# Third block's dense products in a long f32 kernel: seven half-width products for a pair of feature tiles where there were eight

## The reference

```python
def even_layer(h, w_in, conv_w, sgu_ln_g, sgu_ln_b, sgu_w, sgu_b, w_out):
    p = jnp.einsum('bsd,de->bse', h, w_in)
    xa, ba, ca, za, ub, vb, zb = jnp.split(p, EVEN_SPLITS, axis=-1)   # seven parts of 1024
    ya = short_conv_branch(xa, ba, ca, conv_w) * jax.nn.silu(za)      # ba * conv3(ca * xa)
    yb = chunked_sgu_branch(ub, vb, ...) * jax.nn.silu(zb)            # ub * (w_s @ layer_norm(vb) + b_s)
    return jnp.einsum('bse,ed->bsd', jnp.concatenate([ya, yb], axis=-1), w_out)

def odd_layer(h, w_in, ...):
    p = jnp.einsum('bsd,de->bse', h, w_in)
    pc, zc, fd, zd = jnp.split(p, ODD_SPLITS, axis=-1)    # pc: 3200 wide, for a head scan
    ...

def third_block(x, ...):
    h = x
    h = h + even_layer(rms_norm_3(h, e_norm_g), ...)
    h = h + odd_layer(rms_norm_3(h, o_norm_g), ...)
    return rms_norm_3(h, final_norm_g)
```

## Time and profile before

| | us |
|---|---|
| median of 3 runs (lowest to highest) | 5252.62 (5249.73 to 5260.67) |
| the profiled execution's own time | 5247.91 |
| its span, first to last instruction | 5246.1 |
| of it TensorE busy | 4898.0 |
| VectorE busy | 2250.8 |
| ScalarE busy | 886.0 |

### The profile page before, as it was taken

How to read it: one execution, slowest core, us unless ns; L and a number is a source line. 1 busy time by engine, 2 the same in 40 slices (tenths; PEclk the granted TensorE clock), 3 DMA queues, 4 the chain that set the end, 5 groups by cost and what they waited for, 6 DMA issues and landing times.

```text
span 5246.1 us, 54331 instructions
## 1 busy us (share of the span) xinstructions
PE 4898.0 (93%) x23372; PEld 3331.0 (63%) x23372; DVE 2250.8 (43%) x3820; ACT 886.0 (17%) x1530; POOL 146.6 (3%) x228
## 2 busy tenths in 40 slices
PE   8999999889999998999999999899998888888988
PEld 7885445774556885565564788444444777777743
DVE  5674874431214465553441655311011555555402
ACT  0001113120111002212221100100001333333211
POOL 0000000000000000000000000000000111111100
PEclk9998999989999998999999999999999999999999
DMA  6523340013222221112111221222221000000021
GB/s 233 174 88 51 66 71 31 1 33 72 96 73 74 87 91 46 49 41 65 41 33 64 81 89 65 80 74 71 72 72 36 1 1 1 1 1 1 17 91 40
DMA packets 284911, 311.51 MB, mean 59 GB/s; under 512 B 7168, under 2 KB 277632, under 8 KB 281472
## 3 DMA queue, kind: packets, MB, share of 16 engines
q1 hardware_dynamic: 284672, 308.04, 19.9%
HBM read 305.92 MB, written 2.10 MB: 59 GB/s over the span
## 4 chain that ended last, share of the span: by engine, by line
PE 52%; DVE 4%; ACT 3%; issue 0%; DMA 0%; SPq 0%; DVEq 0%; ACTq 0%
PE ps L262 24%; PE ps L338 7%; PE ps L748 4%; PE ps L761 2%; PE ps L735 1%; PE ps L1931 1%; PE ps L2621 1%; PE ps L307 1%; PE ps L456 1%; PE ps L2639 1%; PE ps L768 1%; PE ps L1650 1%; PE ps L2382 1%; PE ps L1639 1%; PE ps L2860 1%; PE ps L2552 1%
## 5 line engine op out<-in xcount | busy, mean ns | idle before, releaser
L262 PE MATMUL ps<-main,w 128*128 128x512 f32 (+1 forms) x4976 | 2161.3, 594 | 71.5 <-DMA w<-in_ffn_wg 19.1
L262 PEld LDWEIGHTS ps<-main,w 128*128 128x128 f32 x4976 | 949.1, 193 | 1206.8 <-issue 1177.2
L338 PE MATMUL ps<-main 128*128 128x256 f32 x2992 | 665.6, 380 | 0.0
L338 PEld LDWEIGHTS ps<-main 128*128 128x128 f32 x2992 | 569.7, 190 | 76.1
L338 PE MATMUL ps<-main,w 128*128 128x256 f32 x2264 | 504.5, 380 | 0.0
L338 PEld LDWEIGHTS ps<-main,w 128*128 128x128 f32 x2264 | 431.1, 190 | 58.8 <-issue 1.4
L748 PE MATMUL ps<-main,w 128*128 128x128 f32 x1536 | 226.5, 297 | 4.0 <-DVE main L2725 2.2
L748 PEld LDWEIGHTS ps<-main,w 128*128 128x128 f32 x1536 | 204.5, 208 | 16.4 <-issue 5.7
L602 DVE SCALAR_TENSOR_TENSOR main<-main,params_sb 128x512 f32<-128x512 f32 x256 | 192.5, 752 | 9.1
L781 ACT COPY main<-ps 128x512 f32<-128x512 f32 x180 | 105.5, 586 | 509.8 <-PE ps L735 509.8
L761 PE MATMUL ps<-main 128*128 128x128 f32 x1440 | 181.9, 280 | 2.4 <-DVE main L807 2.4
(11 more groups left out here) (446 smaller groups left out, 4762.7 us busy)
## 6 DMA issues: line engine op xcount, KB each, us to landing
w<-in_w_in SPq DMA_DIRECT2D x58, 1024.0 KB, 6.2
w<-in_e_w_in SPq DMA_DIRECT2D x28, 1024.0 KB, 5.1
main<-in_ada_w SPq DMA_DIRECT2D x24, 1024.0 KB, 4.9
w<-in_ffn_wg SPq DMA_DIRECT2D x22, 1024.0 KB, 6.3
w<-in_ffn_wu SPq DMA_DIRECT2D x22, 1024.0 KB, 6.4
w<-in_o_w_in SPq DMA_DIRECT2D x20, 1024.0 KB, 5.3
w<-in_ffn_wd SPq DMA_DIRECT2D x16, 1024.0 KB, 5.1
w<-in_w_up SPq DMA_DIRECT2D x16, 1024.0 KB, 5.4
```

Source lines behind the costliest of these rows:

```text
L262: i = pe.mm(PS[b][:, 0:n], wv[:, k, f * 128:(f + 1) * 128], g.X(kg + k), start=kg + k == 0, stop=kg + k == g.nk - 1)
L338: t = pe.mm(PS[b][:, 256 * half:256 * half + 256], weight[:, m, :], x(m), start=m == 0, stop=m == n - 1)
```

## The change

All products of the even layer and p are made by the seven-product step, but for the first pair of v, of x and of p, and p's last single tile, which stay plain. Even input: 26 steps. Even output: the 16 input tiles are taken as two groups of 8 (kg 0 and 8), each a step of its own whose result is added to `X`: 8 steps. p: 11 steps. The order of the input products stays; in the output product groups of 0 and 8 interleave. ScalarE's copies of tiles go, and `act_seven`'s copies come; Silu works on two tiles at once, in place, behind the results. VectorE gets the halves, the weights' differences (made two steps ahead) and the results, which `dve_seven_out` can now write to tiles 514 apart (`stride`).

```diff
-    def dve_seven_out(v, g, j, kg, out):
+    def dve_seven_out(v, g, j, kg, out, stride=TOK):
...
-    G_even = {n: Gemm("even " + n, e_in, k * D, 8, 8, H3, ("rms", "even"))
+    G_even = {n: Gemm("even " + n, e_in, k * D, 8, 8, H3, ("rms", "even"), seven=(*ES, EX, ("even x",)))
...
+    def even_steps():
+
+        e = [(G_even["v"], j, 0) for j in (2, 4, 6)]
+        e += [(G_even[n], j, 0) for j in range(0, 8, 2) for n in "xcbz"][1:]
+        e += [(G_even[n], j, 0) for n in "us" for j in range(0, 8, 2)]
+        return e + [(G_eout, j, kg) for j, kg in ((0, 0), (2, 0), (0, 8), (2, 8), (4, 0), (4, 8), (6, 0), (6, 8))]
...
-        run(pe_gemm(pe, G_even["v"]))
+        steps = even_steps()
+        run(pe_pair(pe, G_even["v"], 0))
+        for step in steps[0:3]:
+            run(pe_seven(pe, *step))
         pe_ln(pe, "sgu", between=lambda pe: run(pe_pair(pe, G_even["x"], 0)))
-        for j in range(0, 8, 2):
-            for n in "xcbz" if j else "cbz":
-                run(pe_pair(pe, G_even[n], j))
+        for step in steps[3:18]:
+            run(pe_seven(pe, *step))
...
+        def silu(g, j):
+            a.wait_ge(*at("out", "seven", 3, g.name, j, 0))
+            a.act(U3.ap, U3.ap, ACT.Silu).then_inc(a.inc(s, "out", g.name, j), 1)
+        for g, j, kg in steps[3:18]:
+            act_seven(a, g, j)
+            if g is G_even["z"]:
+                silu(g, j)
...
+            if g is G_even["c"]:
+                if used:
+                    v.wait_ge(*at(*used))
+                dve_seven_out(v, g, j, 0, 33800)
+                for f in (j, j + 1):
+                    v.wait_ge(*at("out", "even x", f))
+                v.wait_ge(*at("out", "seven", 3, g.name, j, 0))
+                v.tt(src.ap[:, :, 1:513], src.ap[:, :, 1:513], EO, MUL).then_inc(v.inc(s, "even xc", j), 1)
+                v.wait_ge(*at("even xc", j))
+                for f in (j, j + 1):
+                    dve_conv(v, s, ("conv3", f), Y3(f), src(f % 2), 3, lambda i: par("e_conv_w_3", 8 * i + f))
...
+            weights_of(n + 2)
...
+        dve_out = {4: (0, 1), 5: (2, 3), 7: (4, 5)}
+        for n, (g, j, kg) in enumerate(steps[26:], 26):
+            v.wait_ge(*at(*used))
+            dve_seven_out(v, g, j, kg, 33800)
...
+            v.tt(X.ap[:, j:j + 2, :], X.ap[:, j:j + 2, :], EO, ADD).then_inc(v.inc(s, *done, j), 1)
+            v.also(*done, j + 1)
+            used = (*done, j)
+            for f in dve_out.get(n - 26, ()):
+                dve_total_squares(v, "odd", f)
+            weights_of(n + 2)
+        for f in (6, 7):
+            dve_total_squares(v, "odd", f)
...
-        run(pe_gemm(pe, G_p))
+        run(pe_pair(pe, G_p, 0))
+        for j in range(2, 24, 2):
+            run(pe_seven(pe, G_p, j))
+        run(pe_pair(pe, G_p, 24))
```

More of the change, by code:

```diff
@@ L2263, in pe_even @@
             t.then_inc(pe.inc(s, "mm", "sgu", f), 1)
-        run(pe_gemm(pe, G_even["u"]))
-        run(pe_gemm(pe, G_even["s"]))
-        run(pe_gemm(pe, G_eout))
+        for step in steps[18:]:
+            run(pe_seven(pe, *step))
     def act_even(a):
@@ L2270, in act_even @@
         act_rms(a, "even", X, x3)
-        for f in range(8):
+        for f in range(2):
             a.wait_ge(*at("mm", "even v", f))
             a.copy(V3(f), bank("even v", f)).then_inc(a.inc(s, "out", "even v", f), 1)
+        steps = even_steps()
+        for step in steps[0:3]:
+            act_seven(a, *step)
         act_ln(a, "sgu", V3, "e_sgu_ln_g_3", "e_sgu_ln_b_3")
[L2275 to L2287, removed]
+        a.wait_ge(*at("pad3", 0))
+        for f in range(2):
+            a.wait_ge(*at("mm", "even x", f))
+            a.copy(pad3[0].ap[:, f, 1:513], bank("even x", f)).then_inc(a.inc(s, "out", "even x", f), 1)
+        def silu(g, j):
[5 more added lines that the diff above has]
+                silu(g, j)
         for f in range(8):
@@ L2290, in act_even @@
             a.copy(t512[f], bank("sgu tp", f)).then_inc(a.inc(s, "out", "sgu tp", f), 1)
[L2291 to L2294, removed]
+        for g, j, kg in steps[18:26]:
+            act_seven(a, g, j)
+            if g is G_even["s"]:
+                silu(g, j)
+        act_out = {3: (0, 1), 4: (2, 3), 6: (4, 5)}
+        for n, step in enumerate(steps[26:]):
+            act_seven(a, *step)
+            for f in act_out.get(n, ()):
+                act_square(a, "odd", X, x4, f, True)
+        for f in (6, 7):
+            act_square(a, "odd", X, x4, f, True)
     def dve_even(v):
@@ L2350, in assemble @@
     DD, DS, FW = mem(26162, 1, 256), mem(26418, 8), mem(30514, 4, 128)
-    G_p = Gemm("p", o_in, 0, 25, 8, H3, ("rms", "odd"))
+    G_p = Gemm("p", o_in, 0, 25, 8, H3, ("rms", "odd"),
+               seven=([mem(25138 + 2048 * i, 4) for i in range(2)], [mem(29234 + 256 * i, 1, 256)(0) for i in range(2)],
+                      pairs_at(*range(21042, 25138, 1024)), ("odd x",)))
     G_f = Gemm("f", o_in, 4224, 4, 8, H3b, ("rms", "odd 2"))
@@ L2473, in dve_odd @@
         v.fill(PP.ap[:, :, 513:514], 0.0).then_inc(v.inc(s, "pp pad"), 1)
+        for m in range(4):
+            dve_halves(v, ("odd x",), H3, G_p.seven[2], m, ("rms", "odd"))
+        for j in (2, 4):
+            dve_seven_weights(v, G_p, j)
+        for j in range(2, 24, 2):
+            dve_seven_out(v, G_p, j, 0, 8193 + 514 * j, 514)
+            for f in (j, j + 1):
+                v.also("out", "p", f)
+            if j < 20:
+                dve_seven_weights(v, G_p, j + 4)
         v.fence("p")
```

139 lines of the change are left out of this document (95 added, 44 removed).

## The result

The changed kernel takes 5203.52 us (median; 5193.92 to 5205.35), the kernel before, run beside it, 5251.17 (5247.51 to 5260.67). The ratio is 0.9903, interval 0.9885 to 0.9921: 47.7 us faster, where 67.6 were forecast. The direction was right, the size fell short, and the time lies outside the range of 5173 to 5197. The profiled execution took 5202.78 us (span 5201.0), at a granted clock of 0.961 over the span (before 0.966).

The account below looks back on a forecast made before the run. TensorE's streaming was taken as the bound: profiled 5247.9 us - 74.0 for 45 steps + 5.0 for seams + 1.6 for the clock = 5180.5; with the runs' median 4.7 higher, 5185 us was forecast, range 5173 to 5197.

Parts of the forecast that it names:

- The price of a step: Changed products on TensorE: a seven-product step takes 12.09 us, against 13.73 us for a plain pair.
- the saving of 1.64: Each seven-product step in place of a pair saves 1.64 us of TensorE time; 45 steps save 74.0 us.
- all four pieces: TensorE savings: 4.9 us in v, 24.7 in x, c, b, z, 26.3 in u to output product, 18.1 in p.
- the sum: Whole kernel: profiled 5247.9 us less 74.0 saved, plus 5.0 for seams and 1.6 for the clock, makes 5180.5 us.
- The seams: Longer TensorE waits: +0.9 us at v's end, +1.2 at the gating product's start, +2.9 at the output product's end.
- VectorE's room: x, c, b, z rounds: VectorE works 29.9 of 48.4 us; its weight sums are ready 8.4 us early in c.
- The prediction's terms behind c: VectorE work after a c step: last result 0.7, product 1.2, convolution taps 4.0, weight sums 2.8, given as 8.9 us.
- The rival of exposed weight loads: All 45 steps: weight loads don't hide behind matmuls, 131 us lost, 5384 us in all; chance 0.01.
- the clock term: TensorE's clock may fall after v and ahead of the gating product: +1.6 us in all, each between 0 and 3.2.
- the two new gaps: Longer TensorE waits at v's end (2.4 us) and at the gating product's start (+1.2 us), where the clock might fall.
- rival of the falling clock: Clock falls at both gaps, 3.2 us each, and seams cost 7.5 us: 5192 us; chance 0.11.
- what it cost at p's start: Low clock at p's start: first tile took 10.1 us in place of 6.87, so 3.2 us at most per gap.

Follow-up runs that it names:

- p alone: Kernel before with only p in seven-product steps, the even layer left as before; 5243.43 us, ratio 0.9970.
- the first experiment: Changed kernel with ScalarE's first copy of the gating product put ahead of the last Silu of z; 5185.34 us, ratio 0.9863.
- the woven kernel: Changed kernel with the gating product's transpositions and small products put among the steps of x, c, b and z; 5169.73 us, ratio 0.9829.

## Why the prediction missed

**Right.** The price of a step, 12.09, and the saving of 1.64: all four pieces came out within 0.7 us of the sum, and p alone gave the same 18.1. The seams at v's end (+0.8 for 0.9) and at the output product (+2.8 for 2.9; the wait was the 5.1 us that the earlier trace rows had shown for the same shape). VectorE's room: no wait inside a step, and a margin of 8.5 us in three rounds and 6.0 in the first where 8.4 was counted. (The prediction's terms behind c, 0.7 + 1.2 + 4.0 + 2.8, make 8.7 and not 8.9, so its margin is 8.6; and the 0.7 for the results doesn't hold in the first round.) The rival of exposed weight loads fell: no idle time ahead of 7776 records, at loads of 190 ns, and 12.09 us a step. By one sentence of the Trainium skill ("TensorE: Matmul & The Clock Gate", Part 3, The mechanism) these loads would have stood between the matmuls; the measurement decides against it here too. The same section of the Trainium skill also lets a load go ahead of running matmuls into a background weight buffer, and the rows don't speak against that.

**Wrong: the clock term.** The prediction saw that the clock could fall at the two new gaps, took 1.6 us in all, and let each cost 3.2 at most, "what it cost at p's start". Its rival of the falling clock, at 5192, priced it the same way. That row was the wrong one to bound with. At p's start dense pairs follow, and the clock came back within the first pair. At the gating product follow eight rounds of a transposition, a wait of 0.77 and eight small products, and there the clock didn't come back for 24 to 27 us. At 1.2 GHz a round takes 3.67 us (3586.47 to 3590.14 in the chain) and at 2.4 GHz 2.33 (3581.82 to 3584.15 in the first experiment): seven times the 1.34 us between them is the 9.4 us missing there (10.6 less 1.2). A bound from the part's own rounds would have held: eight rounds of 2.33 us, less 0.77 of waiting in each, are 12.5 us of work, and half the clock can add no more than that again. Of the two gaps the prediction held the wrong one for the more likely to fall, too: after v, the wait was 2.3 us and the next two records took 1.10, the full clock. "Against: the gap at the gating product has transposes ahead of it" was an argument that the runs refute: with the transposition ahead of it the clock fell.

The Trainium skill ("TensorE: Matmul & The Clock Gate", Part 1, A second HAM failure mode) tells of a clock that goes up and down where TensorE idles briefly and often between groups of matmuls. The rows here don't show that: with 0.77 us ahead of every group the clock stayed low for 20 to 27 us once it had fallen, and stayed high where it had not fallen.

**Wrong: the scan.** The prediction said that a change of more than 5 us in the head scan would break its sum, and it came: +11.4. The runs show that it takes no new p: the kernel before, with its old p, has 1021.5, and the woven kernel, with the same p as the changed one, 1008.2. (The eight profiles with the new p have 1008.2 to 1028.4, the six with the old one 1007.7 to 1021.5; a small effect of p could hide in that.) The length goes with the granted clock in it, 0.96 at 1008 and 0.94 at 1019 and 1021; what moves that clock from one execution to the next, no run shows. The first profile of before, on which the sum was made, was the shortest of all. The error is to have taken one profiled execution's scan as the fixed part of the sum: against the second profile of before (span 5259.7) the changed kernel's second profile (5191.3) is 68.4 us shorter, against the first (5246.1) its first is 45.1 shorter.

So of the 22.3 us between the sum, 5180.5, and the profiled 5202.8, 11.4 is the scan, 7.8 the clock at the gating product (10.6 less the 1.2 and 1.6 foreseen), 2.4 lies ahead of v, and 0.7 is the low clock's end in the first u step.

**Open.** That the longer wait ahead of the gating product costs the clock there is shown: moving one copy took the loss away, and two idle copies brought it back. What decides whether a wait of 2 us loses the clock is not. What stands ahead may count: seven-product steps in three profiles of three with a loss, plain pairs in three of three without. But six profiles don't rule out the other theory of the expectations, that it hangs on where in time the wait falls, and the executions without a profile can't settle it, since the scan moves their time by as much as a loss does. What stands behind goes with it too, since the clock held behind the seven-product steps of v, through a wait of 2.3 us, where dense work follows (1.10 us for the next two records in all seven profiles with such a v). Why was not tried. Nor is it settled whether a loss at the gating product makes the later scan longer: the four profiles with a loss have scans of 1014.7 to 1028.4, the ten others of 1007.7 to 1021.5, and the two overlap.

## What to carry to other kernels

A step that the kernel already uses elsewhere could be priced here from its own rows to a tenth of a microsecond; what went wrong lay at the end of a dense piece and in a stretch taken as fixed. So list every gap that grows and price it at the lower clock over the whole stretch until dense work comes back, not over the first group behind it. Where a stretch of small products with short waits lies between dense pieces, weave it into them: here that took 18.7 us off, 0.36% of the span, 8.0 of them beyond what moving one copy gave. Before a difference is read off two profiles, look at how long a stretch that wasn't edited takes in each, and profile the kernel before twice.

## What the hardware showed that was not expected

- A first wait of 2.00 to 2.07 us ahead of small products cost some 10 us, by the clock: the part took 28.6 to 29.5 us where it takes 18.8 with a first wait of 0.77. In the kernel with plain pairs ahead, a wait of 2.83 us in place of 0.88 cost 2.
- The head scan of one and the same program took 1007.7 and 1021.5 us in two profiles, at granted clocks of 0.96 and 0.94. This is larger than what several edits of this study were worth.
